# A third pair of one-hot buffers, ten places for gathered rows, and another order on ScalarE and GpSimd in the U stage of an expert layer

## What is computed

```python
def expert_block(args):
    hx, ix, gx = args
    act = jax.nn.gelu(jnp.einsum('tkd,td->tk', u_tab[ix], hx))
    return jnp.einsum('tk,tkd->td', gx * act, v_tab[ix])
```

## Time and profile before

| | us |
|---|---|
| median of 3 runs | 3805.85 |
| lowest, highest | 3803.96, 3814.33 |
| the profiled execution | 3806.96 |
| its span, first to last instruction | 3805.2 |
| mean granted TensorE clock | 0.958 |

### The profile page before, as it was taken

One profiled execution on the slowest core, in us unless ns is written; L12 is line 12 of the kernel. 1 busy time (PEld: TensorE's weight loads), 2 busy tenths in 40 slices (PEclk: granted clock), 3 DMA queues, 4 the chain that ended last, 5 costly groups with the idle time before them and its releaser, 6 DMA issues. The chain is left out here.

```text
span 3805.2 us, 52216 instructions
## 1 busy us (share of the span) xinstructions
PE 3415.7 (90%) x17854; PEld 2993.1 (79%) x17854; DVE 2887.7 (76%) x4884; ACT 1418.4 (37%) x2552; POOL 1770.8 (47%) x1003
## 2 busy tenths in 40 slices
PE   5999969697999999999889899997997998989998
PEld 2998859444999999899888888996776776767776
DVE  4544247595578899998999999657886888878886
ACT  2321135243222222224777777523332333333332
POOL 0000012110211778786888888765554654555510
PEclk8979989798999999999999999998998999999999
DMA  5225334542112778776989888879999999989976
GB/s 197 74 84 180 114 105 144 167 143 80 34 34 66 233 247 257 242 262 230 341 331 348 329 342 334 329 271 356 361 384 358 354 357 353 363 327 375 371 270 210
DMA packets 416593, 947.30 MB, mean 249 GB/s; under 512 B 38035, under 2 KB 230211, under 8 KB 413267
## 3 DMA queue, kind: packets, MB, share of 16 engines
q1 hardware_dynamic: 293252, 457.63, 35.9%
q0 software_dynamic: 114480, 417.47, 29.9%
q10 hardware_dynamic: 8736, 70.78, 4.8%
HBM read 807.65 MB, written 138.11 MB: 249 GB/s over the span
## 5 line engine op out<-in xcount | busy, mean ns | idle before, releaser
L1872 POOL DMA_INDIRECT hT<-peer_v,hT x336 | 595.6, 1773 | 487.3 <-DVE hrow L1884 408.1
L1725 PE MATMUL ps<-h_hi,u_hi 128*128 128x384 f32 x2048 | 699.0, 341 | 31.0 <-POOL u_lo L1611 23.2
L1725 PE MATMUL ps<-h_lo,u_hi 128*128 128x384 f32 x2048 | 689.0, 336 | 0.0
L1725 PE MATMUL ps<-h_hi,u_lo 128*128 128x384 f32 x2048 | 689.0, 336 | 0.0
L1962 PE MATMUL ps<-v_hi,a_hi 128*128 128x512 f32 x1512 | 487.2, 404 | 125.8 <-DVE ga_rest L1896 114.9
L1962 PE MATMUL ps<-vw_rest,a_hi 128*128 128x512 f32 x1512 | 476.4, 397 | 0.0
L1962 PE MATMUL ps<-v_hi,ga_rest 128*128 128x512 f32 x1512 | 474.6, 396 | 0.0
L1962 PEld LDWEIGHTS ps<-v_hi,a_hi 128*128 128x128 f32 x1512 | 283.3, 193 | 219.6 <-DVE vw_rest L1894 147.0
L1842 ACT ACTIVATE v_hi<-vw 128x1024 fp32r<-128x1024 f32 x256 | 270.6, 1057 | 410.9 <-DMA vw<-peer_v 399.1
L1607 POOL DMA_INDIRECT hT<-u_rows,hT x224 | 376.0, 1679 | 95.8 <-issue 51.2
L1884 DVE SCALAR_TENSOR_TENSOR hrow<-hT,dots,hrow 128x1024 f32<-128x1024 f32 x336 | 420.4, 1279 | 0.0
(11 more groups left out here) (336 smaller groups left out, 6040.2 us busy)
## 6 DMA issues: line engine op xcount, KB each, us to landing
vw<-peer_v SPq DMA_DIRECT2D x256, 512.0 KB, 8.5
uw<-u_T SPq DMA_DIRECT2D x128, 512.0 KB, 4.3
s_d<-so SPq DMA_DIRECT2D x256, 192.0 KB, 5.0
gates_d<-big ACTq DMA_DIRECT2D x24, 2048.0 KB, 10.0
gt<-gates_d SPq DMA_DIRECT2D x64, 768.0 KB, 8.8
ga<-s_d SPq DMA_DIRECT2D x256, 192.0 KB, 8.8
wmr<-w_modT SPq DMA_DIRECT2D x32, 512.0 KB, 4.0
tok_d<-st SPq DMA_DIRECT2D x45, 256.0 KB, 2.2
```

The lines of the kernel that those rows point to most:

```text
L1725: mm = pe.matmul(g.ps[4 + 2 * s + b][:, 0:HALF], u[s][:, k, :], h[:, k, b * HALF:(b + 1) * HALF], start=(k == 0 and i == 0), stop=(k == KD ...
L1872: pool.indirect_dma_start(rows[n % NU], None, g.v_rows, bass.IndirectOffsetOnAxis(ap=g.pick[m % GT][:, m // GT:m // GT + 1], axis=0)).then ...
```

## The change

- `R` goes from 2 to 3: three pairs of one-hot buffers. They lie in `hT[:, 0]` to `hT[:, 5]`, and of the row places of this tile only `hT[:, 6]` and `hT[:, 7]` are left; `RING2` goes from 12 to 10. PE's loop over the stage takes three turns at once, so that each product knows its buffer.
- ACT puts the gates of groups 0, 1 and 2 ahead of the stage. In a block it then evacuates and evaluates gelu twice, makes `u_hi(e+2)`, and puts the gates of the two groups 2k + 3 and 2k + 4 last (k is the block's number in the stage).
- POOL does `low(e+2)` ahead of the gathers of turn e. The turns are shifted by one block (to `u_rows_by(e+1)`) and `LEAD` goes from 8 to 4; so, relative to the subtractions, the gathers stand four rows later in the dense stage, and one turn later before it.
- The semaphore `copied` starts at 4, as before, now written as a number.

```diff
-RING1, RING2 = 8, 12
+RING1, RING2 = 8, 10
 U1 = 144
-LEAD = 8
+LEAD = 4
...
-    G, R = 8, 2
+    G, R = 8, 3
...
-            put_gates(0, 0)
-            put_gates(1, 1)
+            for r in range(R):
+                put_gates(r, r)
             for d in range(DENSE):
                 for k in range(BODY):
                     e, s = d * BODY + (H1 + k), k % 2
                     for b in range(2):
-                        q = 2 * k + b
-                        evacuate(d, q)
-                        if d * PER + q + R < TE // G:
-                            put_gates(d * PER + q + R, q % R)
+                        evacuate(d, 2 * k + b)
                         gelu_half(e, s, b)
                     split_u(e + 2, s, d * (BODY // 2) + (H1 + k) // 2 + 1)
+                    for r in range(d * PER + 2 * k, d * PER + 2 * k + 2):
+                        if r + R < TE // G:
+                            put_gates(r + R, r % R)
...
             for e in range(NE):
-                if e < H1:
+                if e < H1 - 1:
                     turn = slots_between(U1, 6, H1 - 4, e)
                 else:
-                    turn = range(min(u_rows_by(e - 1) + (LEAD if e > H1 else 0), GT * NSEL), min(u_rows_by(e) + LEAD, GT * NSEL))
+                    turn = range(min(u_rows_by(e) + (LEAD if e >= H1 else 0), GT * NSEL), min(u_rows_by(e + 1) + LEAD, GT * NSEL))
+                if e + 2 < NE:
+                    low(e + 2)
                 for n in turn:
                     gather(n)
                 for n in slots_between(V1, H2 - 1, NE - 2, e):
                     gather(GT * NSEL + n)
-                if e + 2 < NE:
-                    low(e + 2)
...
-            with pe.Fori(0, DENSE) as d:
-                for k in range(BODY):
-                    e, s = d * BODY + (H1 + k), k % 2
-                    for b in range(2):
-                        product(d, 2 * k + b)
-                        half(e, s, b)
+            with pe.Fori(0, DENSE // R) as m:
+                for c in range(R):
+                    d = m * R + c
+                    for k in range(BODY):
+                        e, s = d * BODY + (H1 + k), k % 2
+                        for b in range(2):
+                            product(d, 2 * k + b, (c * PER + 2 * k + b) % R)
+                            half(e, s, b)
```

More of the change, by code:

```diff
@@ L1439, in row_slot @@
         return 8 + s, c + 1, n - RING2 if c else U1 - 1
-    return s - 4, U1 // RING1 + c + 1, n - RING2 if c else U1 - 1
+    return s - 2, U1 // RING1 + c + 1, n - RING2 if c else U1 - 1
 def hidden_and_gates(nc, g):
-    G, R = 8, 2
+    G, R = 8, 3
     PER = P // G
@@ L1473, in hidden_and_gates @@
         out = [g.big[:, i * P * CT:(i + 1) * P * CT] for i in range(2)]
-        one, two = ([g.hT[:, 2 * i + s, 0:G * P].rearrange("p (g c) -> p g c", c=P) for s in range(R)] for i in range(2))
+        one, two = ([g.hT[:, R * i + s, 0:G * P].rearrange("p (g c) -> p g c", c=P) for s in range(R)] for i in range(2))
         rows = [g.hT[:, i, 0:D] for i in range(RING1)] + [g.big[:, 8192 + i * D:8192 + (i + 1) * D] for i in range(8)]
@@ L1531, in plain @@
                 split_u(e + 2, s, j + 1)
-            act.sem_inc(copied, 2 * R)
+            act.sem_inc(copied, 4)
             act.sem_inc(g_stored[0], 16)
@@ L1570, in _ @@
                     for b in range(2):
-                        q = 2 * k + b
-                        evacuate(d, q)
-                        if d * PER + q + R < TE // G:
-                            put_gates(d * PER + q + R, q % R)
+                        evacuate(d, 2 * k + b)
                         gelu_half(e, s, b)
                     split_u(e + 2, s, d * (BODY // 2) + (H1 + k) // 2 + 1)
+                    for r in range(d * PER + 2 * k, d * PER + 2 * k + 2):
+                        if r + R < TE // G:
+                            put_gates(r + R, r % R)
                     if k % 2 == 1:
-                        act.wait_ge(copied, d * (2 * PER) + 4 * (k + 1) + 2 * R)
+                        act.wait_ge(copied, d * (2 * PER) + 4 * (k + 1) + 4)
                         act.dma_start(g.gates_d[bass.ds(d * 4 + k // 2, 1)].rearrange("o p b t -> p (o b t)"), out[k // 2 % 2]).then_inc(g_stored[k // 2 % 2], 16)
@@ L1731, in hidden, with product @@
                 half(e, s, 1, first)
-            def product(d, q):
+            def product(d, q, pair):
                 r = d * PER + q
@@ L1740, in product @@
                     for c in range(G // 2):
-                        mm = pe.matmul(g.ps[2 * (q % 2) + b][:, c * P:(c + 1) * P], one[q % R][:, b * (G // 2) + c], two[q % R][:, b * (G // 2) + c],
+                        mm = pe.matmul(g.ps[2 * (q % 2) + b][:, c * P:(c + 1) * P], one[pair][:, b * (G // 2) + c], two[pair][:, b * (G // 2) + c],
                                        start=True, stop=True)
```

## The result

The changed kernel took 4033.96 us in the median of four runs (4025.93 to 4042.26), and the kernel before, on the same chip, 3809.82 us in the median of four (3803.96 to 3814.33). The ratio is 1.058, with a 95% interval of 1.056 to 1.060. So it is slower by 224 us where 255 were forecast. The profiled execution took 4025.93 us, 4024.2 of it the span, at a mean granted clock of 0.933. Every ratio in this document compares undisturbed executions alone; one execution of run e3 took 8325 us and does not enter its ratio.

The account below looks back on a forecast made before the run. A ring of waits among four engines over two blocks, 13.6 us a block, was taken as the bound; closing over one, 46 turns of 19.0 plus entry and end add 255 us: 4061 us, 8 in 10 for 4005 to 4135.

Parts of the forecast that it names:

- The bound before, and its ring over two blocks: In the 48 gate-making blocks, waits among ACT, PE, POOL and DVE close over two blocks in 27.7 us: 13.6 a block.
- The ring over one block through the first gather behind the subtraction: In the 48 blocks, lead 4 puts the row ACT's pair 2k+4 needs behind POOL's subtraction, so each block waits; 87%.
- The length of a turn: One block of the 48: subtraction, gather and landing, dot, half a pair, ACT's 7.8 us; in all 19.0 against 13.6.
- the landing: Time for the first gathered row behind a subtraction to arrive: 6.1 us taken, bounds 4.9 and 9.0.
- The entry: Start of the 46 turns: `u_hi(66)` ends at 1796.8, plus 6 us of shift from the blocks before, so 1802.8.
- the part behind the stage: After the 48 blocks, 16 plain blocks and the V stage were forecast to stay as they were.
- the 6 us taken: In the 64 blocks before, the first gather moves 8.3 us later; 6 us reach the dense stage, bounds 0 and 8.3.
- They cost and bring nothing: Third buffer pair and ten places free DVE only from waits it does not have, so no effect on time.
- The store of gates hardly meets the first gather: ACT's 2 MB store, 10 us long, starts 2.4 us after pair 2k+4's gates begin; the gather comes 10.4 us after.
- PE at the low clock: Rival: resting some 6 us a block, PE stays at 1.2 GHz, 24.8 us a block at most: 4328 us; 3%.
- faster: Rival: no ring over one block (lead of five against four); POOL's own 12.9 us a block sets the pace: 3772; 4%.
- The signs: Profile after: subtractions 19 us apart, each waiting for `u_hi`; DVE waits some 8 us, PE rests some 6 us a block.

Follow-up runs that it names:

- e3: Changed kernel with the gates of a block's second pair (2k+4) put behind the next block's first evacuation on ACT; ratio 1.054, 18.02 us a block.
- e8: Changed kernel with LEAD 6 instead of 4; ratio 1.032, 15.55 us a block.
- e1: Changed kernel with LEAD 5 instead of 4, nothing else; ratio 1.034, 16.32 us a block.
- e4: Changed kernel with LEAD 8 instead of 4; ratio 1.004, 13.58 us a block.
- e5: Changed kernel with LEAD 8 and, in the first 63 blocks, GpSimd's old order, gathers ahead of the subtraction; ratio 1.001, 13.59 us a block.
- e2: Kernel before with LEAD 4 instead of 8, nothing else; ratio 1.057, 18.46 us a block.
- e7: Kernel before with the third pair and ten places; lead eight, GpSimd's order and ACT's old order of gates kept; ratio 1.049, 17.47 us a block.
- e6: Changed kernel with three unused copies of 512 columns added on ACT ahead of each block's first evacuation; ratio 1.080, 19.83 us a block.
- e10: Kernel before with the u_lo subtraction moved from GpSimd to VectorE in the stage of 48 blocks; ratio 0.980, 3738.36 us.

## Why the prediction was right, point by point

**The bound before, and its ring over two blocks:** right. e8 and e1 show the same form with leads of six and five, and e4 and e5 show what is behind it: with the ring open the block is 13.58 us against 13.65. The ring had cost the kernel before almost nothing beyond POOL's own work, and each row of lead that is taken away makes it dearer (15.55, 16.32, 18.20).

**The ring over one block through the first gather behind the subtraction:** right, in all 46 turns, and by e2 it is the lead that makes it. ACT's new order only chooses which work lies in the turn.

**The length of a turn:** 19.0 predicted, 18.20 measured. Of its terms, subtraction and the way to the gather were put at 2.55 and are 2.53; dot, half a pair and release 2.41, now 1.15 + 1.25 = 2.40; ACT 7.8, now 7.69. The mis-sized term is the landing: 6.1 taken, and 4.68 and 5.96 in the two turns above, 5.4 on the mean of all 46. The row that I took it from, the first of the earlier trace rows, was issued while DVE worked. My own text had DVE at rest at this point and used that for the subtraction's 2.39, but not for the gather, whose instruction alone is 0.95 us then, where that row's took 1.76. Run e3 fits this: with DVE at work the instruction takes 1.76 and the row is used after 6.4. The landing's 0.7 us and 0.1 from the rounded sum and the small terms make 0.8 a turn, 37 us in 46 turns (874 against 837). The entry takes back 4 of them, and the part behind the stage, 3.4 us shorter, adds as much: 36 us between the forecast span of 4060 and the profiled 4024.2. That the median misses by only 27 is the profiled execution's doing, which was the shortest of the four, 8 us below their median.

**The entry:** predicted `u_hi(66)` at 1802.8, measured 1806.5. The first subtraction ahead of a gather starts at 1266.44, 12.5 us after that of the earlier trace rows: 8.3 by the order, as predicted, and 4.2 by a program that was already later there. DVE's wait for its first row grew from 11.16 to 20.30 us:

```profile
1275.56 2.67 DVE L1632 CUSTOM_DVE_ANT_0 hT<-hT,hrow 128x1024 f32<-128x1024 f32 x1 [20.30 <-DMA hT<-u_rows,hT]
```

The net shift left in the program is near the 6 us taken; e4 against e5 gives 10, with an uncertainty of about as much.

**"They cost and bring nothing", said of the third pair and the ten places:** true of the changed kernel, by e5, which has both and is the kernel before in time. But the reason I gave, that nobody waits for the buffers, does not carry it. In e7, with the old order of gates, the third pair costs 4.9%, since it moves the rows that ACT's list asks for. The step holds only together with gates at the end of the block.

**The store of gates hardly meets the first gather:** as predicted. It is issued at 2200.75 in the turn above, the gather starts at 2211.07, and the page has the store at 7.9 us to landing, where the earlier trace rows has 10.0:

```profile
gates_d<-big ACTq DMA_DIRECT2D x24, 2048.0 KB, 7.9
```

**Rival "PE at the low clock":** it does not bound. PE rests once a block, 4.0 us on the mean (190.1 / 47), less than the 6 expected, because its first product runs at a granted clock of 0.50, 1.2 GHz, after a rest of 5.71 us:

```profile
2204.16 3.79 PE L1741 MATMUL ps<-hT 128*128 128x128 f32 x16 [5.71 <-ACT big L1556]
```

```profile
2204.16:2207.50 3.34, 3.33 (x15) 3.34 (x16) 3.34 (x5) 3.34 (x6) 0.00 (x0) 0.50 0.86 359
```

PE is busy 83 us longer for the same work (674 against 591), 1.7 a block, and still rests 4 of the 18.2 us: the slower products lie in time that it would have waited. e6 decides it: work added to ACT lengthens the block, which it would not if PE were the bound. "TensorE: Matmul & The Clock Gate" of the Trainium skill, Part 1, has the clock fall in rests and come back with work, as these rows do: the next product, at 2212.12, takes 1.95 us again. It has no bearing on the time here.

**Rival "faster":** the point at which it decides was right, a lead of five; the size beyond it was not. At five the ring over one block is gone, but one over two blocks closes, which I had not counted for this rival, and 12.9 us are not reached even at eight. The 12.9 came from one block of the earlier trace rows without a wait, in which a gather fell into a pause of DVE and took 0.94, and e4 shows what POOL takes over a stage: gathers of 1.77 us on the mean (419.6 / 237) and 13.58 us a block.

**The signs:** POOL's wait in every block, subtractions 17.4 to 19.2 us apart, gathers of 0.95 (the fifth of a group in 31 of 46 turns; in the others it meets DVE again and takes up to 1.98), DVE's wait before the first row (7.5 us on the mean where some 8 were forecast), its busy time of 505, and ACT's long wait before the second gates all came. PE's rest is the one that was too large.

## What to carry to other kernels

When engines work down fixed lists, count for each wait how many items have been issued ahead of it and how many the waiting engine's next step needs: between four and five rows of lead lay a ring over one block, and more buffers on one side (e7) can close a ring just as fewer on the other (e2). A new ring is as long as the sum of its pieces, and its landings are to be taken from rows in which the neighbours are in the same state: the other engine at rest or at work, and the same transfers beside them. A ring also sets what meets what, so a new one can bring its own collision, as the store beside e1's first gather. And before a ring is tuned, ask what the shared engine does in it: moving one subtraction of 2.4 us off the engine that gathers gave 1.9%, while no order or buffer tried here gave anything that can be told.

## What the runs showed of the hardware

- **GpSimd and VectorE slow each other.** A gather's instruction takes 0.95 us with VectorE at rest and mostly 1.76 to 1.98 with it at work throughout (in e10 many beside a pair take 0.95 all the same, which stays open); the subtraction 2.39 against 2.9 to 3.4; VectorE's dot product 1.2 against 3.42. The Trainium skill, "SBUF — State Buffer", section "SBUF: two separate sides", says that the two share a pair of ports, and that a VectorE operation with two inputs in SBUF blocks a GpSimd one that reads SBUF, or is blocked by it. The subtraction and the dot product agree with that. For a DMA issued by GpSimd its box speaks of VectorE operations in a 2-port mode, with fp32 copies as the example, and beside these gathers stand pairs and dot products, no copies.
- **An indirect gather beside a large store lands late.** The first gather of 512 KB behind a subtraction is used 4.6 to 6.5 us after its start in the changed kernel, with VectorE mostly at rest, and 6.0 with it at work (e1, first turn). With a store of 2 MB issued 1.0 to 2.1 us behind it, it is used after 11.0 to 12.0 (e1, 23 turns, DVE waiting for it each time).
- **A low granted clock can be free.** The stage ran at 0.88 on the mean, with products at 0.50, and cost no time, as PE was not in the ring.
